# Feature-major projections of a hybrid decoder layer: three 256-column passes per weight tile, read out by VectorE alone

## The chip, the cores and the metric

The kernel runs on one core of one Trainium2 chip. The metric is the device time of one execution in microseconds (us), from the first instruction to the last. Engines are named as in the profile: PE is TensorE's matmuls and PEld its weight loads, DVE is VectorE, ACT is ScalarE, POOL is GpSimd, SP is SyncE, which here only issues DMAs.

## The reference

One decoder layer on 256 tokens of width 4096. What matters here is the input projection, of which most column groups are wanted with features on the partitions ("feature-major"):

```python
u = rmsnorm(h, g_pre)                       # 256 x 4096
p = u @ w_in                                # 4096 x 12296, split into 13 column groups
(fq, fk, fv, fgate, f_logit, sq, sk, sv, sgate, su, ssm_gate, lx, lru_gate) = split(p)
o_fox = forgetting_attention(fq, fk, fv, log_sigmoid(f_logit + b)) * silu(fgate)
o_sb  = stick_breaking_attention(sq, sk, sv) * silu(sgate)
o_ssm = s5_mixer(su, ...) * silu(ssm_gate)          # complex diagonal scan, then a GLU
o_lru = rglru_mixer(lx, ...) * silu(lru_gate)
mixed = concatenate([o_fox, o_sb, o_ssm, o_lru]) @ w_out
return h + rmsnorm(mixed, g_post)
```

All arrays are float32. The kernel splits every float32 operand of a large product into a high part (rounded to the format fp32r, which PE streams in one pass) and a low part (the remainder), and adds three of the four partial products: high by high, high by low and low by high.

## The kernel before, in words

The weights are a list of 32 blocks of 4096 x 512. Each block is cut into 16 chunks (`CH`) of 256 rows, so a chunk is one DMA of 512 KB into one of four ring slots (`RING`). For each chunk ACT writes the high part (`high`, L461) and DVE the low part (`low`, L732), three chunks ahead of PE (`LEAD`). Both wait for the ring slot by the semaphore `w_used`, which PE raises at the end of each chunk.

Twenty of the blocks are feature-major (`chunk_fm`): 4 source blocks (numbers 0 to 3), 8 query and key blocks (4 to 11) and 8 gate blocks (16 to 23). In them the weights are the stationary operand and `acts`, the normalised input with its high part in columns 0 to 255 and its low part in columns 256 to 511 of each k tile, is streamed. A block has four feature tiles `j`, and each tile has a PSUM bank of its own, `main[:, j, :]` with 512 float32 columns. Of each tile and each of the 32 k tiles there is one matmul of 512 columns (high weights by high and low input, L248) and one of 256 (low weights by high input, L250), which lands in the right half of the bank. So the left half holds high by high, and the right half the two cross terms. A chunk has 8 such pairs and a block 128. The other 12 blocks are token-major (`chunk_tm`): the input is stationary, 512 columns of weights are streamed, three matmuls of 512 columns each (L269, L270, L271) into the same columns.

When a feature tile is complete, ACT copies the right half to `cross` (L472, `copy_cross`), and DVE adds the left half to it (L872 in `sum_banks`, L1028 in `gates`) and frees the bank by `bank_free`. When the four tiles are there, DVE multiplies 1024 columns by the norm's factor `rs_row` (L878, L980, L1031). All engines run in program order. On DVE this work stands in the block's last chunk, ahead of `low` of three chunks later.

Work of other kinds lies between the chunks. In the query and key blocks it is the S5 scan: at the start of each block DVE copies parameters (L937, semaphore `p5_ready`), POOL works out phases (L1189 to L1196), ACT takes sines (L555), POOL makes cosines, DVE does the complex products and scans (L950 to L973), and PE multiplies (L324, L339). In the gate blocks it is the attention of two heads a block, started by DVE's copy L1055, followed by POOL (L1224, L1245), PE (L402), and ACT applies SiLU to the four gate tiles (L613).

Of the kernel before, what the change touches and what calls it, by code (L numbers as in the profile page):

```python
# [57 lines left out]
def hybrid_trunk(nc, x, par, bt, ct, wfg, wglu, wri, gpost, wall, out):  # L58
    ctx = ExitStack()
    with ctx:  # L60
# [43 lines left out]
        rs_banks = rs_row.unsqueeze(1).to_broadcast([P, JB, T])  # L104
# [53 lines left out]
        bank_cross = sem("bank_cross")  # L158
# [3 lines left out]
        br_ready = sem("br_ready")  # L162
# [19 lines left out]
        gate_normed, gate_silu, gate_used = sem("gate_normed"), sem("gate_silu"), sem("gate_used")  # L182
# [9 lines left out]
        N_FM = B_V + B_OUT - B_G1  # L192
        V_READ = B_V * JB + (B_G1 - B_V) * TT
        block = ctx.enter_context(nc.Block())
# [43 lines left out]
        def _(pe):  # L238
            def chunk_fm(b, m, c):

                pe.wait_ge(lo_ready, b * CH + c + 1)
                s = c % RING
                for j in range(JB):
                    if c == 0 and not isinstance(m, int):
                        pe.wait_ge(bank_free, m * JB + (j + 1 - JB))
                    for kk in range(KC):
                        k, at = KC * c + kk, kk * BLK + j * P
                        pe.matmul(main[:, j, :], w_hi[:, s, at:at + P], acts[:, k, :],  # L248
                                  start=(k == 0), stop=False)
# [103 lines left out]
            with pe.Fori(0, (B_G1 - B_V) // 2) as ii:  # L353
                for u in range(2):
                    i = ii * 2 + u

                    def v_bank(a):

                        pe.wait_ge(bank_free, (B_V - 1) * JB + 2 * u + a + 1)
                        pe.wait_ge(bank_cross, ii * (2 * TT) + ((B_V - 1) * JB + 2 * u + a + 1))  # L360
# [31 lines left out]
            pe.wait_ge(bank_cross, V_READ)  # L392
            with pe.Fori(0, B_G2 - B_G1) as i:
                for c in range(CH):
# [21 lines left out]
                    chunk_fm(i + B_G1, i + B_V, c)  # L416


            with pe.Fori(0, B_OUT - B_G2) as i:
                for c in range(CH):  # L420
# [16 lines left out]
                    chunk_fm(i + B_G2, i + (B_V + B_G2 - B_G1), c)  # L437


            def out_block(n, u):  # L440

                for c in range(CH):
                    chunk_tm(n + B_OUT, c, 2 * u,
                             lambda a: pe.wait_ge(bank_free, n * TT + (N_FM * JB - 2 * TT + a + 1)),
# [10 lines left out]
        def _(act):  # L455
# [6 lines left out]

            def fm_wait(b, m, j):
                if j < JB - 1:
                    act.wait_ge(fm_done, m * (JB - 1) + j + 1)
                else:
                    act.wait_ge(w_used, b * CH + CH)
# [34 lines left out]
            for c in range(CH):  # L502
# [25 lines left out]
                if c == CH - 1:  # L528
                    copy_cross(0, 0)

            with act.Fori(1, B_QK - B_SRC) as i:
                for c in range(CH):
                    high(i, c + LEAD)
                    if c == CH - 1:
                        copy_cross(i, i)
# [5 lines left out]
            with act.Fori(0, B_V - B_QK) as i:  # L541
                for c in range(CH):
# [18 lines left out]
                    if c == CH - 1:  # L561
                        copy_cross(i + B_QK, i + B_QK)
# [6 lines left out]
            with act.Fori(0, (B_G1 - B_V) // 2) as ii:  # L569
                for u in range(2):  # L570
                    i = ii * 2 + u
                    for c in range(CH):
# [28 lines left out]
                        if c == CH - 1:  # L601
                            for a in range(TT):
                                if a < TT - 1:
                                    act.wait_ge(tm_done, i * (TT - 1) + a + 1)
                                else:
# [3 lines left out]
                                               scale=rstd[:, a:a + 1]).then_inc(bank_cross, 1)  # L609

            def silus(g):
                act.wait_ge(gate_normed, g + 1)
# [14 lines left out]
            with act.Fori(0, B_G2 - B_G1) as i:  # L627
                for c in range(CH):
# [11 lines left out]
                    if c == CH - 1:  # L640
                        copy_cross(i + B_G1, i + B_V)
# [8 lines left out]
            def sb_block(i):  # L650
                for c in range(CH):
# [19 lines left out]
                    if c == CH - 1:  # L671
                        copy_cross(i + B_G2, i + (B_V + B_G2 - B_G1))
# [53 lines left out]
        def _(dve):  # L726
# [141 lines left out]
            def sum_banks(i):  # L868

                for j in range(JB):  # L870
                    dve.wait_ge(bank_cross, i * JB + (j + 1))
                    dve.tensor_tensor(cross[:, j, :], main[:, j, 0:T], cross[:, j, :],  # L872
                                      ALU.add).then_inc(bank_free, 1)

            def source_tiles(i):
                sum_banks(i)
                dve.wait_ge(bank_free, i * JB + JB)
                dve.tensor_tensor(br[:, bass.ds(i * JB, JB), :], cross[:, :, :], rs_banks,  # L878
                                  ALU.mult).then_inc(br_ready, 1)
# [50 lines left out]
            with dve.Fori(0, B_V - B_QK) as i:  # L930
                for c in range(CH):
                    if c == CH - 1:
                        sum_banks(i + B_QK)
# [40 lines left out]
                    if c == CH - 1:  # L974
# [175 lines left out]
            dve.wait_ge(bank_free, N_FM * JB + N_OUT_BLOCKS * TT)  # L1150
# [190 lines left out]
```

## Time and profile before

| | before |
|---|---|
| time of three executions | 1627.17, 1631.53, 1631.62 us; median 1631.53 |
| span of the profiled execution | 1629.7 us |
| PE busy | 1586.2 us (97%) |
| PEld busy | 1331.8 us (82%) |
| DVE busy | 1003.4 us (62%) |
| ACT busy | 820.0 us (50%) |
| POOL busy | 211.2 us (13%) |
| mean granted TensorE clock | 0.996 |

The profile comes from one execution of its own, of which the page gives the span alone, 1629.7 us; the three timed ones lie from 2.5 us below to 1.9 us above it. An engine's busy time is the union of its instructions' records. Matmuls overlap in the record, so PE's share says that PE is hardly ever without work, not how fast it works; that is read from the distance between starts.

### The profile page before, as it was taken

Reading aid. Unit: us, or ns where it says so; the run is one execution under the profiler, and the core shown is the slowest. Engines: PE = TensorE matmul, PEld = TensorE weight load, DVE = VectorE, ACT = ScalarE, POOL = GpSimd, SP = SyncE. Lnnn points to the kernel's source line nnn. Section 1 sums busy time; section 2 is a strip of 40 time slices with the busy share of each in tenths; the row PEclk is TensorE's granted clock in tenths of the full one; section 3 lists DMA queues with packets and bytes.
Section 4 is the critical chain, followed back from the end, with each engine's and each line's share of the span. In section 5 each row is a group of like instructions: output and inputs, shape, how many; then the busy total and the mean of one; then the engine's idle time right before and its main releaser. Section 6 shows DMA issues by size and latency. Waiting matters only on the chain.

```text
span 1629.7 us, 24897 instructions
## 1 busy us (share of the span) xinstructions
PE 1586.2 (97%) x8228; PEld 1331.8 (82%) x8228; DVE 1003.4 (62%) x1237; ACT 820.0 (50%) x1083; POOL 211.2 (13%) x282
## 2 busy tenths in 40 slices
PE   7999999999999999999999999999999999999995
PEld 6888888777877787788888888888888888888884
DVE  6645467987798779545455554556557544444444
ACT  6643334444445444666656453466667544444442
POOL 0000052254235323000001101100000000000000
PEclk9999999999999999999999999999999999999998
DMA  8565635555555555556565545555556876666674
GB/s 291 167 181 169 204 111 171 166 163 163 159 175 151 168 171 164 178 184 196 164 210 158 165 144 187 158 170 177 162 170 187 278 211 193 193 193 193 193 233 154
DMA packets 85574, 294.38 MB, mean 181 GB/s; under 512 B 9504, under 2 KB 11808, under 8 KB 85536
## 3 DMA queue, kind: packets, MB, share of 16 engines
q1 hardware_dynamic: 77184, 276.86, 55.8%
q10 hardware_dynamic: 8352, 17.03, 3.1%
q8 instruction: 22, 0.36, 0.1%
q14 instruction: 16, 0.13, 0.0%
HBM read 289.66 MB, written 4.19 MB: 180 GB/s over the span
## 4 chain that ended last, share of the span: by engine, by line
PE 57%; issue 29%; POOL 6%; DVE 5%; ACT 3%; DVEq 0%; POOLq 0%; ACTq 0%
PE main L248 14%; PE main L269 10%; PE main L270 10%; PE main L271 10%; PE main L250 7%; PE side L374 2%; ACT w_hi L461 1%; POOL scr L1189 1%; DVE vals L961 1%; POOL scr L1192 1%; DVE vals L967 1%; DVE vals L968 1%; POOL scr L1196 1%; POOL scr L1211 1%; POOL scr L1194 1%
## 5 line engine op out<-in xcount | busy, mean ns | idle before, releaser
L732 DVE TENSOR_TENSOR w_lo<-w_raw,w_hi 128x1024 fp32r<-128x1024 f32 x512 | 642.7, 1260 | 528.6 <-ACT w_hi L461 527.6
L248 PE MATMUL main<-acts,w_hi 128*128 128x512 f32 x2560 | 915.9, 401 | 1.2 <-ACT vals L608 1.2
L461 ACT ACTIVATE w_hi<-w_raw 128x1024 fp32r<-128x1024 f32 x512 | 535.2, 1057 | 600.5 <-PE main L250 340.0
L250 PE MATMUL main<-acts,w_lo 128*128 128x256 f32 x2560 | 717.0, 280 | 0.0
L248 PEld LDWEIGHTS main<-acts,w_hi 128*128 128x128 f32 x2560 | 481.7, 188 | 128.9 <-issue 11.1
L250 PEld LDWEIGHTS main<-acts,w_lo 128*128 128x128 f32 x2560 | 484.1, 189 | 0.4
L269 PE MATMUL main<-w_hi,acts 128*128 128x512 f32 x768 | 300.7, 392 | 0.1
L271 PE MATMUL main<-w_hi,acts 128*128 128x512 f32 x768 | 298.9, 389 | 0.0
L270 PE MATMUL main<-w_lo,acts 128*128 128x512 f32 x768 | 298.8, 389 | 0.0
L269 PEld LDWEIGHTS main<-w_hi,acts 128*128 128x128 f32 x768 | 144.2, 188 | 30.5 <-DVE w_lo L732 0.5
L271 PEld LDWEIGHTS main<-w_hi,acts 128*128 128x128 f32 x768 | 144.2, 188 | 30.1
L270 PEld LDWEIGHTS main<-w_lo,acts 128*128 128x128 f32 x768 | 144.2, 188 | 29.7
L1189 POOL TENSOR_TENSOR scr<-scr,small 128x256 f32<-128x256 f32 x32 | 35.6, 1112 | 385.2 <-DVE small L937 385.2
L555 ACT ACTIVATE vals<-scr 128x256 f32<-128x256 f32 x32 | 13.4, 418 | 99.2 <-POOL scr L1196 85.6
L1224 POOL COPY scr<-br 128x256 f32 x16 | 15.6, 972 | 359.3 <-DVE small L1055 324.4
L961 DVE TENSOR_TENSOR_SCAN vals<-small,vals 128x256 f32<-128x256 f32 x64 | 47.7, 785 | 0.0
L324 PE MATMUL side<-scr 128*128 128x256 f32 x128 | 34.6, 393 | 12.6 <-DVE vals L973 12.4
L472 ACT ACTIVATE cross<-main 128x256 f32<-128x256 f32 x80 | 30.5, 381 | 22.8 <-PE main L250 22.0
L872 DVE TENSOR_TENSOR cross<-main,cross 128x256 f32<-128x256 f32 x48 | 20.1, 423 | 29.8 <-ACT cross L472 29.6
L324 PEld LDWEIGHTS side<-scr 128*128 128x128 f32 x128 | 21.7, 189 | 19.7 <-DVE vals L973 17.1
L1228 POOL COPY scr<-vals 128x256 f32 x16 | 7.4, 460 | 204.9 <-PE side L388 204.9
L339 PE MATMUL side<-vals,scr 128*32 128x256 f32 x128 | 33.6, 385 | 0.0
(232 smaller groups left out, 994.3 us busy)
## 6 DMA issues: line engine op xcount, KB each, us to landing
w_raw<-in_wall SPq DMA_DIRECT2D x512, 512.0 KB, 3.6
br<-in_x SPq DMA_DIRECT2D x16, 256.0 KB, 8.0
scr<-in_bt ACTq DMA_DIRECT2D x8, 512.0 KB, 3.3
scr<-in_wglu ACTq DMA_DIRECT2D x8, 512.0 KB, 4.1
out<-br SPq DMA_DIRECT2D x8, 512.0 KB, 3.1
br<-in_gpost ACTq DMA_DIRECT2D x8, 256.0 KB, 5.3
vals<-in_x ACTq DMA_DIRECT2D x8, 256.0 KB, 5.3
scr<-in_x ACTq DMA_DIRECT2D x8, 256.0 KB, 4.6
```

What stands on the lines that cost most here:

```text
L248: pe.matmul(main[:, j, :], w_hi[:, s, at:at + P], acts[:, k, :], start=(k == 0), stop=False)
L250: mm = pe.matmul(main[:, j, T:2 * T], w_lo[:, s, at:at + P], acts[:, k, 0:T], start=False, stop=(k == NK - 1))
L269: pe.matmul(main[:, bank0 + a, :], u_h, wh, start=(k == 0), stop=False)
L270: pe.matmul(main[:, bank0 + a, :], u_h, wl, start=False, stop=False)
L271: mm = pe.matmul(main[:, bank0 + a, :], u_l, wh, start=False, stop=(k == NK - 1))
L324: mm = pe.matmul(side[:, j % 2, r * T:(r + 1) * T], s5_bt[:, j, r, :], s5_u[:, :], start=True, stop=True)
L339: mm = pe.matmul(side[32 * j:32 * j + 32, 2, 0:T], s5_cp[:, j, r, :], s5_h[j % 2][:, r * T:(r + 1) * T], start=(r == 0), stop=(r == 1))
L374: mm = pe.matmul(side[:, 1, 0:T], glu_w[:, k, :], br[:, SSM0 + k, :], start=(k == 0), stop=(k == FT - 1))
L461: act.activation(w_hi[:, c % RING, :], w_raw[:, c % RING, :], ACT.Copy).then_inc(hi_ready, 1)
L732: dve.tensor_tensor(w_lo[:, c % RING, :], w_raw[:, c % RING, :], w_hi[:, c % RING, :].bitcast(F32), ALU.subtract).then_inc(lo_ready, 1)
L961: dve.tensor_tensor_scan(s5_g[:, r * T:(r + 1) * T], radius, s5_m1[:, r * T:(r + 1) * T], 0.0, ALU.mult, ALU.add).then_inc(s5_dve, 1)
L1189: pool.tensor_tensor(s5_a, steps_t, s5_now[:, j:j + 1].to_broadcast([P, T]), ALU.mult).then_inc(s5_tab, 1)
```

## The change

Feature-major blocks no longer keep the cross terms apart. Each weight tile now takes three matmuls of 256 columns into the same 256 PSUM columns: high weights by high input, high weights by low input, low weights by high input. Two feature tiles share a bank (`main[:, pair, half * T:(half + 1) * T]`), so a block uses two banks instead of four. `copy_cross` on ACT and the additions on DVE are gone; DVE multiplies each pair of tiles by `rs_row` directly out of PSUM, 512 columns at a time, once at the middle of the last chunk (`fm_done`) and once at the block's end (`w_used`). The semaphores `bank_cross`, `br_ready` and `gate_normed` are gone, and `bank_free` takes over their counts. The wait for the last value copies (`V_READ`) ahead of the gate blocks is now one for each pair's bank.

```diff
                 for j in range(JB):
-                    if c == 0 and not isinstance(m, int):
-                        pe.wait_ge(bank_free, m * JB + (j + 1 - JB))
+                    pair, half = j // 2, j % 2
+                    if c == 0 and half == 0 and not isinstance(m, int):
+                        pe.wait_ge(bank_free, m * JB + (j + 2 - JB))
+                    tile = main[:, pair, half * T:(half + 1) * T]
                     for kk in range(KC):
                         k, at = KC * c + kk, kk * BLK + j * P
-                        pe.matmul(main[:, j, :], w_hi[:, s, at:at + P], acts[:, k, :],
-                                  start=(k == 0), stop=False)
-                        mm = pe.matmul(main[:, j, T:2 * T], w_lo[:, s, at:at + P], acts[:, k, 0:T],
-                                       start=False, stop=(k == NK - 1))
-                    if c == CH - 1 and j < JB - 1:
+                        pe.matmul(tile, w_hi[:, s, at:at + P], acts[:, k, 0:T],
+                                  start=(k == 0 and half == 0), stop=False, skip_group_check=True)
+                        pe.matmul(tile, w_hi[:, s, at:at + P], acts[:, k, T:2 * T],
+                                  start=False, stop=False, skip_group_check=True)
+                        mm = pe.matmul(tile, w_lo[:, s, at:at + P], acts[:, k, 0:T],
+                                       start=False, stop=(k == NK - 1), skip_group_check=True)
+                    if c == CH - 1 and j == 1:
                         mm.then_inc(fm_done, 1)
...
-            pe.wait_ge(bank_cross, V_READ)
             with pe.Fori(0, B_G2 - B_G1) as i:
...
-            def copy_cross(b, m):
-                for j in range(JB):
-                    fm_wait(b, m, j)
-                    act.activation(cross[:, j, :], main[:, j, T:2 * T], ACT.Copy).then_inc(bank_cross, 1)
...
-            def sum_banks(i):
-
-                for j in range(JB):
-                    dve.wait_ge(bank_cross, i * JB + (j + 1))
-                    dve.tensor_tensor(cross[:, j, :], main[:, j, 0:T], cross[:, j, :],
-                                      ALU.add).then_inc(bank_free, 1)
+            def bank(pair):
+                return main[:, pair, :].rearrange("p (h t) -> p h t", h=2)
+
+            def bank_done(b, m, pair):
+
+                if pair == 0:
+                    dve.wait_ge(fm_done, m + 1)
+                else:
+                    dve.wait_ge(w_used, b * CH + CH)
...
                 for c in range(CH):
                     if c == CH - 1:
-                        sum_banks(i + B_QK)
+                        for pair in range(2):
+                            bank_done(i + B_QK, i + B_QK, pair)
+                            dve.scalar_tensor_tensor(br[:, bass.ds(i * JB + (FOX0 + 2 * pair), 2), :], bank(pair),
+                                                     QK_SCALE, rs_pair, ALU.mult,
+                                                     ALU.mult).then_inc(bank_free, 2)
...
-                        dve.wait_ge(bank_free, i * JB + (B_QK + 1) * JB)
-                        dve.scalar_tensor_tensor(br[:, bass.ds(i * JB + FOX0, JB), :], cross[:, :, :], QK_SCALE,
-                                                 rs_banks, ALU.mult, ALU.mult).then_inc(br_ready, 1)
...
             def gates(i, g, b, tile0):
 
-                for j in range(JB):
-                    dve.wait_ge(bank_cross, g * JB + (V_READ + j + 1))
-                    dve.tensor_tensor(cross[:, j, :], main[:, j, 0:T], cross[:, j, :],
-                                      ALU.add).then_inc(bank_free, 1)
-                dve.wait_ge(bank_free, g * JB + (B_V + 1) * JB)
-                dve.tensor_tensor(cross[:, :, :], cross[:, :, :], rs_banks, ALU.mult).then_inc(gate_normed, 1)
+                for pair in range(2):
+                    bank_done(b, g + B_V, pair)
+                    dve.tensor_tensor(cross[:, 2 * pair:2 * pair + 2, :], bank(pair), rs_pair,
+                                      ALU.mult).then_inc(bank_free, 2)
                 low(b, CH - 1 + LEAD)
```

PE's order before, in a chunk of the query and key blocks: pairs of a wide and a narrow matmul.

```order
L241 REGISTER_ALU
L248 MATMUL main<-acts,w_hi 128x512
L250 MATMUL main<-acts,w_lo 128x256
L248 MATMUL main<-acts,w_hi 128x512
L250 MATMUL main<-acts,w_lo 128x256
```

PE's order after, in the last chunk of a source block (L249, L251 and L253 are the three passes of `chunk_fm`).

```order
L249 MATMUL main<-acts,w_hi 128x256
L251 MATMUL main<-acts,w_hi 128x256
L253 MATMUL main<-acts,w_lo 128x256
L249 MATMUL main<-acts,w_hi 128x256
L251 MATMUL main<-acts,w_hi 128x256
L253 MATMUL main<-acts,w_lo 128x256
L306 REGISTER_ALU
L306 COMPARE_AND_BRANCH
```

Each group of two matmuls has become one of three; every matmul brings a weight load of its own, which these lists don't show. Next, DVE at the end of a query and key block before (L729 and L732 belong to `low`, L976 is S5's output).

```order
L872 TENSOR_TENSOR cross<-main,cross 128x256
L871 REGISTER_ALU
L872 TENSOR_TENSOR cross<-main,cross 128x256
L729 REGISTER_ALU
L732 TENSOR_TENSOR w_lo<-w_raw,w_hi 128x1024
L976 ISA
L976 SCALAR_TENSOR_TENSOR br<-scr,pars,side 128x256
L979 REGISTER_ALU
L980 ISA
L980 SCALAR_TENSOR_TENSOR br<-cross,rs_row 128x1024
L930 REGISTER_ALU
L930 COMPARE_AND_BRANCH
```

And DVE at the same place after (L716 is `low`, L922 the new multiplication out of PSUM, L967 S5's output).

```order
L922 ISA
L922 SCALAR_TENSOR_TENSOR br<-main,rs_row 128x512
L922 ISA
L922 SCALAR_TENSOR_TENSOR br<-main,rs_row 128x512
L713 REGISTER_ALU
L716 TENSOR_TENSOR w_lo<-w_raw,w_hi 128x1024
L967 ISA
L967 SCALAR_TENSOR_TENSOR br<-scr,pars,side 128x256
L917 REGISTER_ALU
L917 COMPARE_AND_BRANCH
```

The four additions and the wide multiplication, which stood behind `low` and S5's output, have become two multiplications ahead of `low`.

## Rows read from the trace of the kernel before

**Rows 1.** The page's first line.

```profile
span 1629.7 us, 24897 instructions
```

**Rows 2.** The page's costliest groups: engine, tiles, shapes, count; busy us, mean ns.

```profile
L248 PE MATMUL main<-acts,w_hi 128*128 128x512 f32 x2560 | 915.9, 401 | 1.2 <-ACT vals L608 1.2
L250 PE MATMUL main<-acts,w_lo 128*128 128x256 f32 x2560 | 717.0, 280 | 0.0
...
L472 ACT ACTIVATE cross<-main 128x256 f32<-128x256 f32 x80 | 30.5, 381 | 22.8 <-PE main L250 22.0
```

**Rows 3.** Line L248 in one source block: count, durations, first and last start.

```profile
L248 PE MATMUL main<-acts,w_hi x129: 395/398/403, 112.0 to 157.2; 128*128 128x512 f32 x129
```

**Rows 4.** Timeline of PE, source block: start us, duration us, instruction.

```profile
133.21 0.40 PE L248 MATMUL main<-acts,w_hi 128*128 128x512 f32 x1
133.44 0.28 PE L250 MATMUL main<-acts,w_lo 128*128 128x256 f32 x1
133.56 0.40 PE L248 MATMUL main<-acts,w_hi 128*128 128x512 f32 x1
...
134.27 0.40 PE L248 MATMUL main<-acts,w_hi 128*128 128x512 f32 x1
```

**Rows 5.** Timeline of PE, gate block: first and ninth L248 of a run.

```profile
925.89 0.40 PE L248 MATMUL main<-acts,w_hi 128*128 128x512 f32 x1
...
928.67 0.40 PE L248 MATMUL main<-acts,w_hi 128*128 128x512 f32 x1
```

**Rows 6.** Line L269 in the token-major output blocks, every third matmul there.

```profile
L269 PE MATMUL main<-w_hi,acts x63: 389/389/390, 1331.6 to 1373.8; 128*128 128x512 f32 x63
```

**Rows 7.** Timeline of weight loads (PEld) for float32 matmuls of 128 columns.

```profile
929.94 0.30 PEld L403 LDWEIGHTS side<-later,scr 128*128 128x128 f32 x2
930.16 0.10 PEld L404 LDWEIGHTS side<-causal_b,ident_b 128*128 128x128 bf16 x1
```

**Rows 8.** PE's waits: total us, times, longest us.

```profile
PE side L324 <- DVE vals L973: 12.4, 8, 1.8
...
PE side L402 <- POOL scr L1245: 1.2, 3, 0.5
PE main L248 <- ACT vals L608: 1.2, 1, 1.2
```

**Rows 9.** Timeline of PE around the S5 wait of the second query block.

```profile
289.80 0.28 PE L250 MATMUL main<-acts,w_lo 128*128 128x256 f32 x1
...
291.86 0.70 PE L324 MATMUL side<-scr 128*128 128x256 f32 x2 [1.78 <-DVE vals L973]
```

**Rows 10.** Timelines of ACT, then DVE, at the end of the block before.

```profile
268.85 0.38 ACT L472 ACTIVATE cross<-main 128x256 f32<-128x256 f32 x1 [0.33 <-PE main L250]
...
269.60 1.21 DVE L732 TENSOR_TENSOR w_lo<-w_raw,w_hi 128x1024 fp32r<-128x1024 f32 x1
...
271.13 1.22 DVE L980 SCALAR_TENSOR_TENSOR br<-cross,rs_row 128x1024 f32 x1
272.26 1.22 DVE L732 TENSOR_TENSOR w_lo<-w_raw,w_hi 128x1024 fp32r<-128x1024 f32 x1
273.64 0.18 DVE L937 TENSOR_SCALAR small<-scr 128x20 f32 x1 [0.16 <-DVE w_lo L732]
```

**Rows 11.** DVE's groups: a product of 512 columns read from PSUM.

```profile
L950 DVE TENSOR_TENSOR vals<-side,vals 128x512 f32<-128x512 f32 x32 | 21.8, 680 | 0.0
```

**Rows 12.** Timelines of DVE and ACT behind the first gate block's end.

```profile
918.54 0.42 DVE L1028 TENSOR_TENSOR cross<-main,cross 128x256 f32<-128x256 f32 x1 [0.27 <-ACT cross L472]
...
920.26 1.06 ACT L613 ACTIVATE cross<-cross 128x1024 f32<-128x1024 f32 x1 [0.45 <-DVE cross L1031]
...
924.87 0.16 DVE L1055 TENSOR_SCALAR small<-scr 128x4 f32 x1
```

**Rows 13.** Timeline where the value blocks end and the gate blocks begin.

```profile
866.71 0.69 ACT L608 ACTIVATE vals<-main,small 128x512 f32 x1 [0.67 <-PE main L271]
...
867.75 0.49 PE L248 MATMUL main<-acts,w_hi 128*128 128x512 f32 x1 [1.18 <-ACT vals L608]
```

More of the change, by code:

```diff
@@ L103, in hybrid_trunk @@
         s5_cos = [vflat[:, 3584:3840], vflat[:, 3840:4096]]
-        rs_banks = rs_row.unsqueeze(1).to_broadcast([P, JB, T])
+        rs_pair = rs_row.unsqueeze(1).to_broadcast([P, 2, T])
         rs_diag = scr[:, 3072:3328]
@@ L181, in hybrid_trunk @@
         sb_act, sb_dve = sem("sb_act"), sem("sb_dve")
-        gate_normed, gate_silu, gate_used = sem("gate_normed"), sem("gate_silu"), sem("gate_used")
+        gate_silu, gate_used = sem("gate_silu"), sem("gate_used")
         mix_hi, mix_lo = sem("mix_hi"), sem("mix_lo")
@@ L191, in hybrid_trunk @@
         LRU_AT = (1, 8)
-        N_FM = B_V + B_OUT - B_G1
         V_READ = B_V * JB + (B_G1 - B_V) * TT
+        M_GATE = V_READ // JB
+        FREE_OUT = V_READ + (B_OUT - B_G1) * JB
         block = ctx.enter_context(nc.Block())
@@ L357, in v_bank @@
                     def v_bank(a):
-                        pe.wait_ge(bank_free, (B_V - 1) * JB + 2 * u + a + 1)
-                        pe.wait_ge(bank_cross, ii * (2 * TT) + ((B_V - 1) * JB + 2 * u + a + 1))
+                        pe.wait_ge(bank_free, (B_V - 1) * JB + 2 * (a + 1))
+                        pe.wait_ge(bank_free, ii * (2 * TT) + (B_V * JB - 2 * TT + 2 * u + a + 1))
                     for c in range(CH):
@@ L415, in _ @@
                             weighted_values(h)
-                    chunk_fm(i + B_G1, i + B_V, c)
+                    chunk_fm(i + B_G1, i + M_GATE, c)
             with pe.Fori(0, B_OUT - B_G2) as i:
@@ L436, in _ @@
                             weighted_values(h)
-                    chunk_fm(i + B_G2, i + (B_V + B_G2 - B_G1), c)
+                    chunk_fm(i + B_G2, i + (M_GATE + B_G2 - B_G1), c)
             def out_block(n, u):
@@ L443, in out_block @@
                     chunk_tm(n + B_OUT, c, 2 * u,
-                             lambda a: pe.wait_ge(bank_free, n * TT + (N_FM * JB - 2 * TT + a + 1)),
+                             lambda a: pe.wait_ge(bank_free, n * TT + (FREE_OUT - 2 * TT + a + 1)
+                                                  if u or not isinstance(n, int) else FREE_OUT - JB + 2 * (a + 1)),
                              mixed_parts=isinstance(n, int) and n == 0)
@@ L866, in take_low @@
                                          acts[:, k, 0:T].bitcast(F32), ALU.mult, ALU.subtract).then_inc(u_lo, 1)
-            def sum_banks(i):
-                for j in range(JB):
-                    dve.wait_ge(bank_cross, i * JB + (j + 1))
-                    dve.tensor_tensor(cross[:, j, :], main[:, j, 0:T], cross[:, j, :],
-                                      ALU.add).then_inc(bank_free, 1)
+            def bank(pair):
[5 more added lines that the diff above has]
+                    dve.wait_ge(w_used, b * CH + CH)
             def source_tiles(i):
[L876 to L879, printed above, removed]
+                for pair in range(2):
+                    bank_done(i, i, pair)
+                    dve.tensor_tensor(br[:, bass.ds(i * JB + 2 * pair, 2), :], bank(pair), rs_pair,
+                                      ALU.mult).then_inc(bank_free, 2)
             dve.wait_ge(par_in, 16)
@@ L1024, in gates @@
             def gates(i, g, b, tile0):
-                for j in range(JB):
-                    dve.wait_ge(bank_cross, g * JB + (V_READ + j + 1))
-                    dve.tensor_tensor(cross[:, j, :], main[:, j, 0:T], cross[:, j, :],
-                                      ALU.add).then_inc(bank_free, 1)
-                dve.wait_ge(bank_free, g * JB + (B_V + 1) * JB)
-                dve.tensor_tensor(cross[:, :, :], cross[:, :, :], rs_banks, ALU.mult).then_inc(gate_normed, 1)
+                for pair in range(2):
+                    bank_done(b, g + B_V, pair)
+                    dve.tensor_tensor(cross[:, 2 * pair:2 * pair + 2, :], bank(pair), rs_pair,
+                                      ALU.mult).then_inc(bank_free, 2)
                 low(b, CH - 1 + LEAD)
@@ L1149, in _ @@
             root(fin_dve, 1, slice(0, TT))
-            dve.wait_ge(bank_free, N_FM * JB + N_OUT_BLOCKS * TT)
+            dve.wait_ge(bank_free, FREE_OUT + N_OUT_BLOCKS * TT)
             for a, q in quarters:
@@ L1226, in fetch_values @@
             def fetch_values(h):
-                pool.wait_ge(bank_cross, V_READ)
+                pool.wait_ge(bank_free, V_READ)
                 pool.tensor_copy(at_v, vals[:, :, bass.ds(h * P, P)]).then_inc(vs_ready, 1)
```

19 lines of the change are left out of this document (2 added, 17 removed).

## The prediction

> **What bounds the kernel now.** I read the page first: a span of 1629.7 us [rows 1], in which the two matmuls of the feature-major blocks, 2560 of each, are the largest items [rows 2]. Their mean durations (401 and 280 ns) overlap, so they are no price; the price is the distance between starts. PE's own waits are the next view, and they are small: 12.4 us for the S5 scan, 1.2 us for POOL in the attention stage, 1.2 us for ACT's value copies [rows 8]. So the end is set by how fast PE gets through its columns. Everything that the change takes from ACT and DVE matters only through those few waits, while every nanosecond on a feature tile's group of matmuls counts 2560 times.
>
> **The pace of a pair now.** In a source block 129 starts of L248 lie between 112.0 and 157.2 us [rows 3]: 45.2 us over 128 intervals is 353 ns a pair. Three pairs in detail give 1.06 us, again 353 ns, of which the wide matmul holds 0.23 and the narrow one 0.12 us before the next start [rows 4]. In a gate block eight pairs take 2.78 us, 347 ns [rows 5]. Both paces occur in the query, key and gate blocks, so I take 350 ns there, and 353 ns for the 512 pairs of the source blocks. In the token-major blocks, where all matmuls have 512 columns, 62 intervals of three take 42.2 us: 227 ns each [rows 6].
>
> **What a 256-column matmul costs in a row of its kind.** The trace before doesn't show one; the narrow matmul always follows a wide one. At 2.4 GHz 512 columns are 213.3 ns and 256 are 106.7 ns. The token-major matmul has 13.4 ns above that. Give each matmul of a pair the same surplus, and the pair is 213.3 + 106.7 + 26.8 = 346.8 ns, which is the gate block's 347 without a remainder. If the surplus grew with columns instead, the pair would be 1.5 x 227 = 340 ns, which neither stage reaches. So I read the surplus as one for each matmul with its weight load: 120 ns for 256 columns, 360 ns for three. The bounds: by the columns alone 113 ns (340 for three, the floor); by the distance behind the narrow matmul 117 to 120 ns (351 to 360), but that distance and the one before it only mean something as a sum; by the source stage's surplus, (353 - 320) / 2 = 16.7 ns, 123 ns (370); and if a narrow matmul's place is all that a pair has beyond 227 ns in the source stage, 353 - 227 = 126 ns (379, the ceiling). The surplus is there three times instead of twice, and that is the whole loss.
>
> Can the third weight load be hidden? A float32 tile of the same size was loaded twice in 0.22 us, from 929.94 to the next load at 930.16 [rows 7], 110 ns each, under matmuls of 128 columns. So a load fits under 120 ns, with 10 ns to spare. The Trainium skill ("TensorE: Matmul & The Clock Gate", Back-to-back issue gap) gives N/2.4 + 2.5 ns for a warm stream: 109 ns for 256 columns, 328 ns for three, and with it 58 us less than now. The same formula would make the token-major matmul 216 ns, and this trace has 227, so the formula's fixed part does not hold for these operands; I keep it as a remote rival.
>
> The rate term: 512 x (360 - 353) + 2048 x (360 - 350) = 3.6 + 20.5 = **+24 us**.
>
> **What the shorter read-out gives back.** Removed are 80 copies of ACT (381 ns each [rows 2]) and DVE's 80 additions; the 1024-column multiplications become two of 512 columns from PSUM, 0.68 us each by the nearest row [rows 11]. In the source blocks this is worth nothing: PE doesn't wait there, and DVE and ACT have time left. Three places remain.
>
> Query and key blocks: PE stands still before L324 in the middle of a block, from 289.80 to 291.86 [rows 9], 2.06 us between starts where 0.12 is usual. It waits for the first of four S5 steps, and that chain begins with DVE's L937 at the block's start. PE finished the previous block at 268.8 (ACT's last copy starts at 268.85); DVE then did the addition, `low` (269.60), S5's output, the wide multiplication (271.13), `low` again (272.26) and L937, which ended at 273.82 [rows 10]: 5.0 us behind PE. After the change DVE starts the second multiplication at once (0.05 + 0.65), then `low` 1.2, S5's output 0.4, `low` 1.25 and L937 0.3: 3.8 us. The chain of POOL, ACT and DVE behind it starts 1.2 us earlier, and so does its end. PE comes later by itself: some seven chunks of 8 groups at 10 ns are 0.5 us. The wait shrinks by 1.7 of its 1.9 us in seven blocks, -12 us. The first of the eight blocks starts behind the forget-gate products and not behind this tail, so there only PE's later arrival counts: -0.5 us.
>
> Gate blocks: DVE's last addition starts 918.54, SiLU 920.26 and L1055 924.87 [rows 12]. PE was done at about 918.1 (that addition less a copy of 0.38 [rows 2]), and only one 0.68 us product would stand between it and SiLU, so SiLU starts 1.4 us earlier, and `high`, `low` and L1055 behind it move too. PE's three waits at L402, none over 0.5 us [rows 8], disappear: -1.2 us.
>
> Start of the gate blocks: PE waited 1.18 us for ACT's last value copy [rows 13]. Now only the second bank's does, 1.4 us into the chunk, when the copy (866.71 + 0.69) is done: -1.3 us.
>
> The new waits cost nothing while DVE is on time. The first bank's product starts in the middle of the last chunk, 1.4 us before PE comes back to it, and takes 0.68 us; the second bank's starts at the block's end, and PE comes back to it 1.4 us later. Each is free 0.7 us early. What is queued behind DVE's wait for the block's end is `low` of two chunks on, and it now starts at 0.7 instead of 0.8 us. Were DVE 1 us late, that cover would be gone and 0.3 us a block lost, 6 us over 20.
>
> Sum: +24 - 12 - 0.5 - 1.2 - 1.3 = **+9 us**. The span was 1629.7 and the median of the runs is 1631.5, 1.8 us above it; I put the sum on the median: **1640 us**. With 1.3 ns either way on a matmul (10 us on 2560 groups) this case reaches from 1630 to 1650.
>
> **The rivals.**
> - *The narrow matmul keeps its 117 ns.* Three take 351 ns: 512 x (-2) + 2048 x 1 = +1 us, and the read-out gives back 8.4 (7 x 1.2) + 1.2 + 1.3 = 11: 1622 us, the other side. For it: that is the distance shown [rows 4]. Against it: the wide one's 0.23 is above 227 ns, so some of its time is the narrow one's. It decides from about 118.8 ns a matmul downwards: gains of 15 us, divided by 7680 matmuls, are 2 ns, and today's pair is 3 x 116.9 ns on the mean of all stages.
> - *The surplus goes by columns.* 340 ns: 512 x (-13) + 2048 x (-10) = -27 us, -11 for the read-out, +4 since PE arrives earlier at the S5 waits: 1597 us. Against it are both paces. The page's 109 ns would go further, to about 1565.
> - *A weight load under every 256 columns adds stalls*, or the source stage's larger surplus is what dense loads bring: 370 ns, 512 x 17 + 2048 x 20 = +50 us, less 16: 1665 us. At the ceiling of 379: 512 x 26 + 2048 x 29 = +73, less 17: 1688 us. For it: the pair had one load per 384 columns, the new group one per 256, and the margin to the shown 110 ns is thin.
> - *PE's instruction supply becomes the bound*: three matmuls and loads where two were. Against it, the two loads in 0.22 us came from a stream as dense as the new one [rows 7], though a short one. It would look like the case before.
>
> **How the numbers follow.** 360 ns: 0.42. 351 ns: 0.22. Near 340 or below: 0.11. 370 ns and above: 0.25, of which 0.07 beyond 1667. The range 1614 to 1667 leaves out the columns case and the far end of the stalls, together under 0.2. A difference of 0.3%, 5 us, is about what a measurement of this kernel can tell from no change. Faster: the two fast cases and a little of the first, 0.34. Same: 0.14, the lower part of the 360 ns case. Slower: 0.52.
>
> **What would show it.** Starts of L249 in a source block 360 ns apart and matmuls 120 ns; if 117 or 123, the rate step is wrong in that direction and by 7.7 us for each ns. Source blocks 46.1 us instead of 45.2. The gap before the S5 matmuls near 0.3 us; if it still is 1.9 us, the chain doesn't hang on DVE's tail. No PE wait for the value copies, and no wait of L249 for DVE's new products. The prediction fails most surely by the pace of one matmul, since it counts 7680 times.

## The result, and the profile after

The changed kernel takes 1637.72 us (median of 5 runs, 1636.97 to 1639.23), the kernel before 1631.33 (5 runs): a ratio of 1.004, interval 1.0028 to 1.0052, or +6.4 us where +9 was forecast. The profiled execution's span is 1637.5 us, against 1629.7 [rows 1].

The page of the changed kernel, first line, engines, and the groups that answer to [rows 2] (busy us, mean ns; PEld is the weight load):

```profile
span 1637.5 us, 29726 instructions
...
PE 1606.9 (98%) x10788; PEld 1473.1 (90%) x10788; DVE 974.3 (59%) x1177; ACT 792.8 (48%) x1003; POOL 208.2 (13%) x282
...
L249 PE MATMUL main<-acts,w_hi 128*128 128x256 f32 x2560 | 736.2, 288 | 0.2 <-DVE br L865 0.2
L253 PE MATMUL main<-acts,w_lo 128*128 128x256 f32 x2560 | 725.2, 283 | 0.0
L251 PE MATMUL main<-acts,w_hi 128*128 128x256 f32 x2560 | 725.2, 283 | 0.0
```

The three groups look alike, and their mean durations (pipeline depth included) still say nothing of the pace. That stands in the distance of the starts, here line L249 in the source block of [rows 3]: count, durations, first and last start.

```profile
L249 PE MATMUL main<-acts,w_hi x129: 283/283/283, 114.8 to 160.9; 128*128 128x256 f32 x129
```

128 intervals in 46.1 us are 360 ns a group, where [rows 3] give 353. PE's timeline shows it matmul by matmul, then the S5 place of [rows 9], then the first L404 of the first gate block (start us, duration us):

```profile
130.30 0.28 PE L249 MATMUL main<-acts,w_hi 128*128 128x256 f32 x1
130.42 0.28 PE L251 MATMUL main<-acts,w_hi 128*128 128x256 f32 x1
130.54 0.28 PE L253 MATMUL main<-acts,w_lo 128*128 128x256 f32 x1
130.66 0.28 PE L249 MATMUL main<-acts,w_hi 128*128 128x256 f32 x1
...
294.91 0.28 PE L253 MATMUL main<-acts,w_lo 128*128 128x256 f32 x1
295.19 0.70 PE L327 MATMUL side<-scr 128*128 128x256 f32 x2
...
877.70 0.28 PE L253 MATMUL main<-acts,w_lo 128*128 128x256 f32 x1
878.84 0.37 PE L404 MATMUL side<-br,scr 128*128 x1 [0.86 <-POOL scr L1231]
```

A start every 120 ns, three to a group. The S5 matmul follows 0.28 us behind the last L253, and no releaser stands behind it: the gap of 2.06 us in [rows 9] is gone. The last row is new: 0.86 us of waiting for POOL in the first gate block, where before only blocks 1 to 3 waited. The list of PE's waits, in answer to [rows 8] (total us, times, longest us):

```profile
PE side L371 <- DVE scr L993: 1.0, 1, 1.0
PE side L404 <- POOL scr L1231: 0.9, 1, 0.9
PE side L327 <- DVE vals L964: 0.5, 1, 0.5
PE side L371 <- DMA scr<-in_wri: 0.5, 1, 0.5
PE main L249 <- DVE br L865: 0.2, 1, 0.2
```

12.4 us in eight S5 waits have become 0.5 us in one. DVE's tail of a query block, in answer to [rows 10]; the last L253 of this block starts at 273.03 and ends at 273.31:

```profile
273.48 0.69 DVE L922 SCALAR_TENSOR_TENSOR br<-main,rs_row 128x512 f32 x1 [0.73 <-PE main L253]
274.08 1.22 DVE L716 TENSOR_TENSOR w_lo<-w_raw,w_hi 128x1024 fp32r<-128x1024 f32 x1
275.22 0.47 DVE L967 SCALAR_TENSOR_TENSOR br<-scr,pars,side 128x256 f32 x1
275.61 1.22 DVE L716 TENSOR_TENSOR w_lo<-w_raw,w_hi 128x1024 fp32r<-128x1024 f32 x1
276.98 0.18 DVE L928 TENSOR_SCALAR small<-scr 128x20 f32 x1 [0.15 <-DVE w_lo L716]
```

L928, with which the S5 chain starts, ends at 277.16, 3.85 us behind PE. It was 5.0 before, and 3.8 was forecast.

By stages, from the first feature-major matmul of one to that of the next: the source blocks and the forget gate became 4.1 us longer (0.5 of it ahead of their first matmul), the first query block 0.4 longer, query and key blocks 1 to 6 are 4.9 shorter (54.47 instead of 55.28 us each), the last of them with the value blocks 1.1 shorter, the first gate block 2.5 longer, gate blocks 1 to 6 are 5.8 longer, the rest 0.9. That is +7.7 us, the difference of the spans but for rounding. So every stage with feature-major blocks pays the rate, and the query and key blocks from the second on alone get more back than they pay.

### The profile page after: what moved, and what is told of

Read it like the earlier page. It is cut to its first block, busy times and chain, and to the rows that moved or that the text cites. A ratio compares the mean times of both kernels' runs of the same rounds, so it can differ in the third digit from the quotient of the medians.

```text
span 1637.5 us, 29726 instructions
## 1 busy us (share of the span) xinstructions
PE 1606.9 (98%) x10788; PEld 1473.1 (90%) x10788; DVE 974.3 (59%) x1177; ACT 792.8 (48%) x1003; POOL 208.2 (13%) x282
## 4 chain that ended last, share of the span: by engine, by line
PE 83%; issue 14%; DVE 1%; POOL 1%; DMA 0%; ACT 0%; DVEq 0%; ACTq 0%; POOLq 0%
PE main L249 15%; PE main L251 14%; PE main L253 14%; PE main L272 10%; PE main L274 10%; PE main L273 10%; PE side L342 2%; PE side L327 2%; PE side L377 2%; DVE br L1140 1%; DMA scr<-in_wri 0%; PE side L371 0%; PE side L390 0%; PE side L407 0%; PE side L431 0%
## 5 line engine op out<-in xcount | busy, mean ns | idle before, releaser
L716 DVE TENSOR_TENSOR w_lo<-w_raw,w_hi 128x1024 fp32r<-128x1024 f32 x512 | 643.0, 1259 | 552.4 <-ACT w_hi L464 551.5
L249 PE MATMUL main<-acts,w_hi 128*128 128x256 f32 x2560 | 736.2, 288 | 0.2 <-DVE br L865 0.2
L253 PE MATMUL main<-acts,w_lo 128*128 128x256 f32 x2560 | 725.2, 283 | 0.0
L251 PE MATMUL main<-acts,w_hi 128*128 128x256 f32 x2560 | 725.2, 283 | 0.0
L249 PEld LDWEIGHTS main<-acts,w_hi 128*128 128x128 f32 x2560 | 491.8, 192 | 16.0 <-issue 9.9
L251 PEld LDWEIGHTS main<-acts,w_hi 128*128 128x128 f32 x2560 | 492.0, 192 | 0.5
L253 PEld LDWEIGHTS main<-acts,w_lo 128*128 128x128 f32 x2560 | 491.8, 192 | 0.0
L543 ACT ACTIVATE vals<-scr 128x256 f32<-128x256 f32 x32 | 13.4, 418 | 97.2 <-POOL scr L1182 84.6
L1182 POOL TENSOR_TENSOR scr<-scr 128x256 f32<-128x256 f32 x32 | 32.5, 1016 | 2.5
```

The costliest lines, as they stand in the source:

```text
L249: pe.matmul(tile, w_hi[:, s, at:at + P], acts[:, k, 0:T], start=(k == 0 and half == 0), stop=False, skip_group_check=True)
L251: pe.matmul(tile, w_hi[:, s, at:at + P], acts[:, k, T:2 * T], start=False, stop=False, skip_group_check=True)
L253: mm = pe.matmul(tile, w_lo[:, s, at:at + P], acts[:, k, 0:T], start=False, stop=(k == NK - 1), skip_group_check=True)
L716: dve.tensor_tensor(w_lo[:, c % RING, :], w_raw[:, c % RING, :], w_hi[:, c % RING, :].bitcast(F32), ALU.subtract).then_inc(lo_ready, 1)
```

## The experiments

**1. The split alone.** (The code in each experiment is a cut from its edit, with arguments left out.) The kernel before, with its wide matmul cut into two of 256 columns; outputs, accumulation and the whole read-out as before.

```diff
-pe.matmul(main[:, j, :], w_hi[:, s, at:at + P], acts[:, k, :], ...)
+pe.matmul(main[:, j, 0:T], w_hi[:, s, at:at + P], acts[:, k, 0:T], ...)
+pe.matmul(main[:, j, T:2 * T], w_hi[:, s, at:at + P], acts[:, k, T:2 * T], ...)
```

> The kernel before, of which only the 512-column matmul of each feature tile is split into two of 256 columns, left and right half of the bank; copies, additions and multiplications stay. Theory (a surplus of 13.3 ns above its columns for every matmul with its weight load): starts 120 ns apart, 360 ns a group instead of 347 to 353, so +24 us of rate, of which the S5 waits hide about 4: 1631 + 20 = 1651 us, and those waits shrink from 1.9 to about 1.4 us. Rival (the 120 ns of the changed kernel come from accumulating three times in a row into the same columns): here only the second and third pass share columns, the group takes 350 ns or less, 1631 us. Second rival (the weight load, not the matmul, sets 120 ns): the same as the theory here.

Measured: 1646.34 us (4 runs) against 1631.21, ratio 1.0098 (1.0081 to 1.0115). PE's timeline at the S5 place of the second query block:

```profile
294.12 0.28 PE L252 MATMUL main<-acts,w_lo 128*128 128x256 f32 x1
295.58 0.48 PE L326 MATMUL side<-scr 128*128 128x256 f32 x1 [1.18 <-DVE vals L975]
```

Groups start 360 ns apart here too, so the pace is a matter of the number of matmuls; that all three go to the same PSUM columns costs nothing, and neither does the read-out. The wait is still there, 0.5 us shorter than before: PE comes later. Rate +22.8, the eight S5 waits 3.6 shorter together (12.4 to 8.8) and L402's waits gone (-1.2) make +18; the spans differ by 16.0. The expectation had 24 for the rate and -4 for the S5 waits; it left out L402's waits, and the second S5 place of each block, where a group now takes 2.32 us instead of 2.46 to 2.62 (-1.5 beyond the rate in eight blocks).

**2. The read-out alone.** The changed kernel with the two matmuls of before; the read-out takes columns 0 to 255 of each bank, so the cross terms are left out of the feature-major results.

```diff
-pe.matmul(tile, w_hi ...) ; pe.matmul(tile, w_hi ...) ; pe.matmul(tile, w_lo ...)
+pe.matmul(main[:, j, :], w_hi[:, s, at:at + P], acts[:, k, :], ...)
+mm = pe.matmul(main[:, j, T:2 * T], w_lo[:, s, at:at + P], acts[:, k, 0:T], ...)
...
-return main[:, pair, :].rearrange("p (h t) -> p h t", h=2)
+return main[:, 2 * pair:2 * pair + 2, 0:T]
```

> The changed kernel with the matmuls of before (512 and 256 columns, four banks); DVE reads the left halves of two banks at a time in the two multiplications, so the cross terms are left out of the feature-major columns. Theory: the pace is that of before, 347 to 353 ns a pair, and only the read-out's gain is left: seven S5 waits shrink by 1.2 us each, the waits for POOL and for the value copies go, 11 us in all: 1620 us. Rival (the shorter read-out gives nothing, and the small loss of the change is due to a smaller rate term): 1631 us, S5 gaps still 1.9 us.

Measured: 1620.89 us (6 runs), ratio 0.9944 (0.9929 to 0.9959); the profiled span is 1617.1. Timeline of PE at the same place, and then PE's waits:

```profile
287.44 0.28 PE L250 MATMUL main<-acts,w_lo 128*128 128x256 f32 x1
288.33 0.70 PE L324 MATMUL side<-scr 128*128 128x256 f32 x2 [0.61 <-DVE vals L961]
```

```profile
PE side L324 <- DVE vals L961: 3.8, 8, 0.9
...
PE side L401 <- POOL scr L1228: 1.1, 1, 1.1
```

The short read-out takes the S5 waits from 12.4 to 3.8 us with the matmuls of before; the later arrival of PE in the changed kernel takes the rest, as it took 3.6 us in experiment 1. That 1620 was met so closely is in part luck: in this profiled execution the pairs of source blocks 1 to 3 run 347 ns apart and not 353, which makes 2.6 us that the forecast gain of 11 doesn't contain (experiment 4 comes back to it). This gain and the first experiment's loss are the two halves of the change: -10.3 and +15.1 us by the medians are +4.8, where the whole change measured +6.4.

**3. The moved multiplication.** Of the kernel before, only L980 (the wide multiplication ahead of the S5 chain) is moved: it runs behind L938 of the next block, and once more after the loop, whose first block is written out for it. The cut shows the line taken out and the call put in.

```diff
-dve.scalar_tensor_tensor(br[...], cross[:, :, :], QK_SCALE, rs_banks, ...).then_inc(br_ready, 1)
...
+if not (isinstance(i, int) and i == 0):
+    scaled(i - 1)
```

> The kernel before with one edit: in the query and key blocks DVE's 1024-column multiplication is done in the next block, behind the copies that start the S5 chain, instead of at the block's end. Theory (that chain hangs on DVE's tail): L937 comes 1.2 us earlier in seven blocks, each S5 gap falls from 1.95 to 0.75 us, 8.4 us in all: 1623 us. Rival (the chain is set by ACT's sines and POOL, whose start is bound elsewhere, or the deferred 1.2 us comes back on DVE in front of the low parts): 1631 us.

Measured: 1636.89 us (8 runs), ratio 1.0036 (1.0023 to 1.005): 0.4% slower, where 1623 was expected. Timelines of POOL, DVE and PE; the S5 chain begins with POOL's row at 274.61:

```profile
274.61 0.64 POOL L1198 TENSOR_TENSOR scr<-scr,small 128x256 f32<-128x256 f32 x1 [23.84 <-DVE small L941]
275.33 1.48 POOL L1201 TENSOR_TENSOR scr<-scr,small 128x256 f32<-128x256 f32 x1
276.88 0.61 POOL L1203 TENSOR_TENSOR scr<-scr,small 128x256 f32<-128x256 f32 x1
...
272.95 1.23 DVE L732 TENSOR_TENSOR w_lo<-w_raw,w_hi 128x1024 fp32r<-128x1024 f32 x1 [0.55 <-ACT w_hi L461]
274.70 1.64 DVE L931 SCALAR_TENSOR_TENSOR br<-cross,rs_row 128x1024 f32 x1
...
402.32 0.28 PE L250 MATMUL main<-acts,w_lo 128*128 128x256 f32 x1
404.56 0.70 PE L324 MATMUL side<-scr 128*128 128x256 f32 x2 [1.96 <-DVE vals L979]
```

Two things took the gain. DVE's `low` now waits 0.55 us for ACT, which reads out the cross terms and loads a table before it makes `high`, so the chain started 0.5 us earlier and not 1.2. And the moved multiplication (1.64 us instead of 1.22) now stands beside POOL's three operations, and the one that meets it takes 1.48 us instead of about 0.61. In three of the seven later blocks something else followed the gap; stretches of one such block (start and end, length, busy PE, PEld, DVE, ACT, POOL, granted clock, DMA share, GB/s):

```profile
382.00:405.00 23.00, 21.04 (x118) 18.10 (x117) 17.45 (x20) 11.93 (x17) 16.79 (x20) 1.00 0.53 165
405.00:410.00 5.00, 5.00 (x18) 2.74 (x17) 4.97 (x6) 2.40 (x5) 3.17 (x5) 0.66 0.35 105
```

Up to 404.56 PE had started nothing for 2.24 us; behind it the granted clock is 0.66 over 5 us, part of the stretch at the lower level (1.2 GHz). The three blocks with such a stretch lost 1.0 to 1.4 us each beyond their longer gap. One more stands ahead of all this, in block 0, where nothing was edited (clock 0.76 over 62 to 66): by the starts it cost 1.5 of the 7.8 us between the profiled spans. So the run refutes the size that the theory gave and doesn't test its place, which experiment 7 does: a step taken out of DVE's tail comes back where it lands.

**4. The order of the old pair.** The kernel before, with the two k tiles of a feature tile as wide, narrow, narrow, wide.

```diff
-for kk in range(KC):
+for kk, part in ((0, "wide"), (0, "narrow"), (1, "narrow"), (1, "wide")):
```

> The kernel before, with the four matmuls of a feature tile and chunk in the order wide, narrow, narrow, wide instead of wide, narrow, wide, narrow. Theory (each matmul has 13.3 ns above its columns, and the 353 ns of the source blocks are a disturbance of the strict alternation): 693 ns for two pairs in all stages, so 347 instead of 350.6 on average, 9 us less, of which the S5 waits take back about 3: 1625 us. Rival (353 ns come from what ACT, DVE and DMA do meanwhile, or go with every change of width): as before, 1631 us, or more if two narrow ones in a row cost more than 240 ns.

Measured: 1628.62 us (12 runs), ratio 0.999 (0.9981 to 1.0), span 1625.9. The interval touches 1.0, and the 1625 that was expected is missed. PE's timeline (equal neighbours are one row, x2):

```profile
133.43 0.39 PE L252 MATMUL main<-acts,w_lo 128*128 128x256 f32 x2
133.66 0.63 PE L249 MATMUL main<-acts,w_hi 128*128 128x512 f32 x2
134.12 0.40 PE L252 MATMUL main<-acts,w_lo 128*128 128x256 f32 x2
```

Two pairs take 0.69 to 0.70 us, 348.5 ns a pair, in every stage; a source block takes 44.6 us instead of 45.2. The gate blocks had 349.1 already, and what the query and key blocks gain in pace (351.5 to 348.5) their S5 waits take back in part (12.4 to 13.1 us). So the 353 ns of the source stage are not the price of dense loads, which are the same here. But the order alone doesn't make them either. Line L248 in a source block of experiment 2, wide and narrow in strict turn:

```profile
L248 PE MATMUL main<-acts,w_hi x128: 391/391/391, 111.8 to 155.9; 128*128 128x512 f32 x128
```

127 intervals in 44.1 us are 347 ns, and so it is in experiment 8, whose source blocks are those of the kernel before to the letter. What chooses between 347 and 353 is open.

**5. Each scheme where it pays.** Source and gate blocks as in experiment 4, query and key blocks as in the changed kernel; the whole computation.

> Source and gate blocks as before the change (wide and narrow matmuls, copies, additions), but in the order wide, narrow, narrow, wide; only the eight query and key blocks take three 256-column passes and the short read-out. Theory (the change pays only where the S5 waits are, and costs 7 to 13 ns a group elsewhere): the query and key blocks take 54.47 us as in the changed kernel instead of 55.25, 5.5 us in all, and the source blocks 2.5 us less by the order: 1631 - 8 = 1623 us, faster than both kernels. Rival (the gain is given back behind the S5 stage, as the gain at the value copies was): 1629 us or more.

Measured: 1623.37 us (6 runs, 1622.84 to 1625.0) against 1630.91, ratio 0.9958 (0.9945 to 0.9972), the fastest full version of the study. PE's waits:

```profile
PE side L428 <- POOL scr L1274: 1.6, 3, 0.5
...
PE side L350 <- DVE vals L1005: 0.5, 1, 0.5
```

The S5 waits are those of the changed kernel, the waits of the gate stage those of experiment 4 (1.6 us in three; 1.2 before [rows 8]). The shorter read-out is kept only for the 1024 groups whose tail PE waits for.

**6. Other widths.** One look: in source blocks 1 to 3 six matmuls of 128 columns a group, in gate blocks 0 to 3 two of 384, the low one of them 128 columns off, so that the gate values there aren't the reference's.

```diff
+[("hi", 128 * n, 128 * n, 128) for n in range(4)] + [("lo", 256 + 128 * n, 128 * n, 128) for n in range(2)]
...
+[("hi", 0, 0, 384), ("lo", 128, 0, 384)]
```

> The kernel before with other widths in two stages. Source blocks 1 to 3: six matmuls of 128 columns for each feature tile and k tile, the same sums. Gate blocks 0 to 3: two of 384 columns, of which the low-weight one lands 128 columns off, so that the gates' values are not the reference's. Theory (columns at 2.4 GHz plus 13.3 ns for each matmul): 80 ns for 128 columns, 480 ns a group; 173.3 ns for 384, 347 ns a group without the 353 ns of the alternating widths. Rival (a weight load needs about 107 to 110 ns, so that this is the floor, and the 120 ns at 256 columns are near it): about 110 ns for 128 columns, 660 ns a group, and 1631 + 384 x 0.31 = 1750 us; 384 columns as the theory.

Measured: 1754.7 us, a single run. A window of 60 us in the source blocks (columns as above), and PE's timeline in a gate block:

```profile
130.00:190.00 60.00, 60.00 (x540) 60.00 (x539) 17.13 (x17) 13.19 (x15) 0.00 (x0) 1.00 0.33 97
```

```profile
997.80 0.33 PE L251 MATMUL main<-acts,w_hi 128*128 128x384 f32 x1
...
1000.75 0.33 PE L251 MATMUL main<-acts,w_lo 128*128 128x384 f32 x1
```

17 intervals in 2.95 us are 173.5 ns for 384 columns, 13.5 above their 160 ns at 2.4 GHz; 256 columns have 13.3 above 106.7, the token-major 512 columns 13.4 above 213.3 [rows 6]. So the surplus belongs to the matmul and not to its columns. At 128 columns it fails: 53.3 + 13.3 would be 67 ns, and 540 matmuls in 60 us are 111 ns. That the weight load sets this pace fits the loads of [rows 7], 110 ns apart, but isn't shown apart from other limits. PEld's busy share, 60.00 of 60.00 us here, says nothing on it. The same view of the changed kernel, in whose source blocks matmuls start 120 ns apart:

```profile
120.00:150.00 30.00, 30.00 (x253) 30.00 (x252) 12.56 (x11) 11.00 (x11) 0.00 (x0) 1.00 0.65 193
```

PEld is busy throughout there too, since its records (192 ns each) overlap.

**7. The cover of the S5 wait.** The changed kernel with an unused multiplication of 1024 columns on DVE at the end of each query and key block, where L980 stood.

```diff
+dve.tensor_tensor(cross[:, :, :], br[:, LRU0:LRU0 + JB, :], rs_row..., ALU.mult)
```

> The changed kernel, with one more multiplication of 1024 columns (1.22 us, its result is used by nobody) on DVE at the end of each query and key block, where the kernel before has its own. Theory (the S5 chain hangs on DVE's tail): the gap ahead of the S5 matmuls in the middle of a block goes from 0.28 to about 1.45 us, as in the kernel with only the split matmuls, 7 x 1.2 = 8 us more: 1646 us. Rival (ACT's earlier table load, which came with the missing copies, is what moved the chain): the gap stays at 0.3 to 0.8 us and the time at 1638 to 1641 us.

Measured: 1645.19 us (5 runs), ratio 1.0093 (1.0077 to 1.0108). PE's timeline:

```profile
294.05 0.28 PE L253 MATMUL main<-acts,w_lo 128*128 128x256 f32 x1
295.47 0.70 PE L327 MATMUL side<-scr 128*128 128x256 f32 x2 [1.14 <-DVE vals L964]
```

An operation of about 1.2 us on DVE brings back 1.14 us of waiting on PE in each of the seven blocks, 8 us, and the median rises by 7.5. PE's wait hangs on DVE's tail nearly one for one, and the change leaves it next to no margin.

**8. DVE beside POOL.** The kernel before with the same unused multiplication right behind L938, beside POOL's first operations of the S5 chain and not ahead of them.

```diff
+dve.tensor_tensor(cross[:, :, :], br[:, LRU0:LRU0 + JB, :], rs_banks, ALU.mult)
```

> The kernel before, with one more multiplication of 1024 columns on DVE (SBUF to SBUF, its result is used by nobody) right behind the copies that start the S5 chain, where e3_defer put its deferred one; the block's own multiplication stays at its end. Theory (in e3_defer the multiplication ran beside POOL's first phase operations and stretched one of them from 0.61 to 1.48 us, since both engines were in SBUF): POOL's phase ends 0.9 us later, the S5 gaps go from 1.95 to 2.8 us, and where PE stands still that long the clock falls for some microseconds; 8 x 0.9 = 7 us and more: 1638 to 1650 us. Rival (POOL isn't touched by it and e3_defer lost its time elsewhere): DVE is idle for 5 us there, so 1631 us.

Measured: 1645.78 us (5 runs), ratio 1.0088 (1.0074 to 1.0102). Timelines of POOL, DVE and PE:

```profile
273.89 0.65 POOL L1190 TENSOR_TENSOR scr<-scr,small 128x256 f32<-128x256 f32 x1 [24.32 <-DVE small L937]
274.62 1.47 POOL L1193 TENSOR_TENSOR scr<-scr,small 128x256 f32<-128x256 f32 x1
...
273.99 1.63 DVE L939 TENSOR_TENSOR cross<-br,rs_row 128x1024 f32<-128x1024 f32 x1
...
347.58 0.28 PE L250 MATMUL main<-acts,w_lo 128*128 128x256 f32 x1
350.16 0.70 PE L324 MATMUL side<-scr 128*128 128x256 f32 x2 [2.30 <-DVE vals L974]
```

POOL's second operation began inside DVE's (274.62, while DVE ran until 275.62) and ended 0.47 us behind it; it took 1.47 us, and the gap before S5 grew from about 1.95 to 2.43 to 2.58 us. The Trainium skill ("SBUF — State Buffer", Who interferes with whom) says that GpSimd and a DVE instruction of this kind share ports under an exclusive lock, so that the later one stands until the earlier is through. By that rule POOL's operation would end about its own time behind DVE's end, and the trace agrees roughly: 0.47 us, with 0.61 for the undisturbed one. The eight S5 waits grew by 5.0 us (12.4 to 17.4); the median rose by 15 and the profiled span by 13.2. Most of the rest is the clock (0.82 over 404 to 412, 0.99 over the whole span). In five of the seven later query and key blocks it fell behind the gap, and these lost 1.4 to 1.7 us each beyond the gap, 8.0 together; the two in which it stayed up lost at most 0.4. A stretch at the lower level in block 0 is in this trace too (0.71 over 62 to 66; the block is 1.8 us longer), and source blocks 1 to 3, at 347 ns a pair, give 2.6 us back.

## Why the prediction was right

**The pace.** The step "120 ns for 256 columns, 360 ns for three" held in all stages (359.6 to 360.0 ns), and the reading under it, a surplus for each matmul, held for 256, 384 and 512 columns. What I took for the pace before was off in places: 353.3 in the source blocks, 351.5 in the query and key blocks, 349.1 in the gate blocks, where I had 353, 350 and 350. Rate term: 3.4 + 8.4 + 11.0 = 22.8 us, predicted 24. So the two halves of the 20.5 were 10.2 each where 8.4 and 11.0 came, and the errors partly cancel. The rival of 117 ns fell with experiment 1, that of a surplus by columns (340, or 328 by the formula of the Trainium skill, "TensorE: Matmul & The Clock Gate", Back-to-back issue gap) with the same row. That section calls its formula the gap of an isolated matmul; in the dense stream here the part above the columns is 13.3 ns and not 2.5. Stalls did not come at 256 columns; at 128 the pace is 111 ns, near the 110 ns of [rows 7].

**The S5 waits.** Predicted -12 and -0.5. By the waits they are 12.4 us before and 0.5 after, so -11.9. The chain was read rightly: 3.85 us behind PE where 3.8 was forecast, a gap of 0.28 us where 0.3 was. Experiments 2 and 7 move it from both sides.

**The attention stage.** Predicted -1.2. The three waits at L402 went, and by the starts they were worth more than the list says: the groups around them take 2.03 us instead of 2.83, 2.63 and 2.63, which is -2.0. (The list counts idle time from the end of a matmul, 0.28 us behind its start, while the next one of a stream would have started after 0.12.) But the first gate block has a new wait at L404, +1.1 by the starts. POOL and DVE there, before and after:

```profile
876.95 0.40 POOL L1245 TENSOR_TENSOR scr<-later,small 128x128 f32<-128x128 f32 x1
877.55 1.23 DVE L732 TENSOR_TENSOR w_lo<-w_raw,w_hi 128x1024 fp32r<-128x1024 f32 x1 [0.82 <-ACT w_hi L461]
...
876.54 1.42 DVE L716 TENSOR_TENSOR w_lo<-w_raw,w_hi 128x1024 fp32r<-128x1024 f32 x1
876.84 1.38 POOL L1231 TENSOR_TENSOR scr<-later,small 128x128 f32<-128x128 f32 x1
```

POOL's chain starts at the same time as before (DVE's L1041 at 874.00, L1055 at 874.10). PE, which had lost its wait for the value copies, came 1.1 us earlier, freed the ring slot earlier, and so ACT's `high` and DVE's `low` came earlier too; that `low` now stands beside POOL's second product, which takes 1.38 us instead of 0.40 and ends the chain 0.9 us later. In the other eight traces it is the same: 1.38 us where PE came early (experiments 2 and 7), 0.40 where it still waited for the value copies (experiments 1, 3 to 6 and 8). So net -0.9.

**The value copies.** Predicted -1.3, and the wait of 1.18 us [rows 13] did go, 1.3 by the starts. Most of it came back: in the wait at L404 as told, and 0.9 us by the starts at L371 in the value stage (waits of 1.5 us in two places instead of 0.7 in one). Of that last part 0.5 us is a wait for a transfer that experiment 7, with the same value stage, doesn't have, so it may not belong to the change. This step failed: I removed a wait without asking what PE would meet next, and what its earlier `low` would run beside. Its size is about a microsecond.

**New waits** for DVE's products: predicted none, measured one of 0.2 us (L249, behind source block 0).

**What the sum left out.** The list of terms had nothing for four places, read here by the starts: the second S5 place of a query and key block, 2.32 us instead of 2.46 in six blocks and 2.6 in two (-1.5 beyond the rate); a wait of 0.6 us for ACT at L380 in the last gate block, now gone (-0.7); a wait at L298 (L301) in block 0, 0.2 shorter; and the first matmul, 0.5 later.

Rate +22.8, S5 -11.9 and -1.5, the waits at L402 and L404 -0.9, the value stage -1.3 + 0.9, L380 -0.7, L298 -0.2, the new wait +0.2 and the later start +0.5: +7.9, where the spans differ by 7.7. The forecast of +9 had the two large terms right to about a microsecond each, and the small ones it missed have both signs.

## What to carry to other kernels

A stream of matmuls is priced by the distance between starts, and splitting one in two costs the surplus of one more matmul (13.3 ns here), although not a column is added; find it from rows of two widths, and multiply by the count. A shorter read-out is worth only what the engine that sets the end waits for it: decide stage by stage, as experiment 5 did, and not for all blocks. And of each wait that is removed, ask which fixed event comes next and what the work it releases will run beside; of each operation that is moved, what runs beside it where it lands.

## What the runs showed of the hardware

- For these operands a matmul with a weight tile of its own takes its columns at 2.4 GHz plus 13.3 to 13.5 ns: 120 ns for 256, 173.5 for 384, 226.7 for 512. At 128 columns it is 111 ns, near the distance of two weight loads (110 ns).
- Wide and narrow in turn run at 347 or 353 ns a pair over long stretches; as wide, narrow, narrow, wide they hold 348.5. The source blocks, in the same order, had 353 in the kernel before and 347 in experiments 2 and 8. Open why.
- A POOL operation of 0.61 us took 1.47 and 1.48 us beside a DVE operation of 1024 columns in SBUF, and DVE's took 1.63 instead of 1.22. In the first gate block one of 0.40 us took 1.38 beside `low`, which took 1.42 instead of 1.23.
- Where PE started nothing for 2.15 to 2.6 us ahead of the S5 matmuls, the granted clock fell in some blocks (three of seven in experiment 3, five of seven in experiment 8); at 1.8 to 2.1 us, in the kernel before and in experiment 4, in none. The length of the gap isn't all: ahead of L298 in block 0 PE started nothing for 2.4 us (58.30 to 60.74) in the kernel before, which kept 1.00 over 62 to 66, and as long in experiment 3, which had 0.76. What else it takes is open. A fall cost 1.0 to 1.7 us.
